# A decoder step on one core: seven half-tile products in place of eight in the up projection of the second token half

## What is computed

```
g = x @ w_gate                       # 1024 x 2816
g_c = depthwise_causal_conv(g, w_dw) # 3 taps along the tokens
y = (gelu(g_c) * (x @ w_up)) @ w_down
```

## Time and profile before

| what | us |
|---|---|
| median of 3 runs (lowest, highest) | 3045.91 (3045.04, 3047.52) |
| span of the profiled execution | 3046.1 |
| PE busy | 3011.0 |
| DVE, ACT, POOL busy | 1858.8, 1354.2, 406.6 |
| up projection of half 1, each layer | 264.2 |

### The profile page before, as it was taken

How to read it: one execution, slowest core, us unless ns; L and a number is a source line. 1 busy time by engine, 2 the same in 40 slices (tenths; PEclk the granted TensorE clock), 3 DMA queues, 4 the chain that set the end, 5 groups by cost and what they waited for, 6 DMA issues and landing times.

```text
span 3046.1 us, 62013 instructions
## 1 busy us (share of the span) xinstructions
PE 3011.0 (99%) x24682; PEld 2625.4 (86%) x24682; DVE 1858.8 (61%) x2754; ACT 1354.2 (44%) x2427; POOL 406.6 (13%) x602
## 2 busy tenths in 40 slices
PE   8999999999999999999999999999999999999998
PEld 7887888888999998998777777777798888999998
DVE  6998677744655445534666666666567763555522
ACT  5344633333333333323676777776543333333322
POOL 0112000000000002220433333433100000000000
PEclk9999999999999999999999999999999999999999
DMA  4232233334333335556999999999623333333332
GB/s 132 72 86 79 84 90 97 97 107 121 98 97 91 90 105 182 177 164 213 344 390 404 396 404 395 404 403 393 229 84 97 97 95 113 113 105 89 89 109 85
DMA packets 483249, 534.60 MB, mean 176 GB/s; under 512 B 22241, under 2 KB 400474, under 8 KB 482888
## 3 DMA queue, kind: packets, MB, share of 16 engines
q1 hardware_dynamic: 467254, 482.90, 46.8%
q0 software_dynamic: 15616, 47.55, 4.7%
q10 hardware_dynamic: 92, 0.19, 0.0%
HBM read 486.84 MB, written 33.89 MB: 171 GB/s over the span
## 4 chain that ended last, share of the span: by engine, by line
PE 86%; DVE 9%; ACT 2%; issue 2%; DMA 1%; SPq 0%; DVEq 0%; ACTq 0%
PE PS L1149 59%; PE PS L2273 7%; PE PS L2309 4%; PE PS L2285 4%; DVE mT L952 4%; PE PS L2328 2%; PE PS L2347 2%; PE PS L2338 2%; DVE wlo L380 1%; PE PS L669 1%; ACT whi L375 1%; PE PS L1800 1%; PE PS L713 0%; PE PS L1022 0%; PE PS L623 0%
## 5 line engine op out<-in xcount | busy, mean ns | idle before, releaser
L375 ACT CAST whi<-raw 128x1024 fp32r<-128x1024 f32 (+1 forms) x368 | 379.5, 1031 | 917.9 <-PE PS L1149 884.2
L380 DVE TENSOR_TENSOR wlo<-raw,whi 128x1024 fp32r<-128x1024 f32 (+1 forms) x368 | 442.7, 1203 | 556.5 <-ACT whi L375 543.4
L1149 PE MATMUL PS<-xfh,whi 128*128 128x512 f32 (+2 forms) x2240 | 618.9, 327 | 1.0 <-DVE wlo L380 0.9
L1149 PE MATMUL PS<-xfh,wlo 128*128 128x512 f32 (+2 forms) x2240 | 615.2, 326 | 0.0
L1149 PE MATMUL PS<-xfl,whi 128*128 128x512 f32 (+2 forms) x2240 | 613.5, 325 | 0.0
L1149 PEld LDWEIGHTS PS<-xfh,whi 128*128 128x128 f32 x2240 | 379.1, 188 | 35.5 <-issue 3.4
L1149 PEld LDWEIGHTS PS<-xfl,whi 128*128 128x128 f32 x2240 | 379.6, 188 | 32.4 <-issue 0.5
L1149 PEld LDWEIGHTS PS<-xfh,wlo 128*128 128x128 f32 x2240 | 378.5, 188 | 33.0
L2273 PE MATMUL PS<-ident,kr 128*128 128x128 f32 x2048 | 277.3, 276 | 2.6 <-ACT kt L2443 2.6
L2273 PEld LDWEIGHTS PS<-ident,kr 128*128 128x128 f32 x2048 | 224.7, 140 | 39.0 <-issue 37.2
L2536 DVE COPY kt<-PS 128x512 f32<-128x512 f32 x256 | 172.6, 681 | 129.8 <-PE PS L2273 128.1
(11 more groups left out here) (380 smaller groups left out, 5348.6 us busy)
## 6 DMA issues: line engine op xcount, KB each, us to landing
kr<-in_cache_k SPq DMA_DIRECT2D x256, 512.0 KB, 7.5
vr<-in_cache_v SPq DMA_DIRECT2D x256, 512.0 KB, 7.2
raw<-in_ffn_w_gate SPq DMA_DIRECT2D x88, 512.0 KB, 3.8
raw<-in_ffn_w_up SPq DMA_DIRECT2D x88, 512.0 KB, 3.8
raw<-in_ffn_w_down SPq DMA_DIRECT2D x64, 512.0 KB, 3.7
raw<-in_ffn_w_down SPq DMA_DIRECT2D x32, 384.0 KB, 3.4
raw<-in_conv_w_glu SPq DMA_DIRECT2D x16, 512.0 KB, 4.2
raw<-in_conv_w_out SPq DMA_DIRECT2D x16, 512.0 KB, 3.7
```

The lines of the kernel that those rows point to most:

```text
L375: nc.scalar.copy(whi[b][:, 0:blocks_of(t), :], raw[t % RAWS][:, 0:blocks_of(t), :]).then_inc(w_hi, 1)
L380: nc.vector.tensor_tensor(wlo[t % RAWS][:, 0:n, :], raw[t % RAWS][:, 0:n, :], whi[b][:, 0:n, :].bitcast(F32), ALU.subtract).then_inc(w_lo, 1)
L1149: mm = nc.tensor.matmul(PS[:, s + c, 0:c1 - c0], stationary(wt, t, kw + k), x(k0 + k)[:, c0:c1], start=start and k == 0 and wt is whi and ...
```

## The change

Blocks 3 to 19 of half 1 in both layers are worked as a pair of tiles: the 2 x 2 matrix of weight quarters (A11, A12 the gate tile's row blocks 0 to 3 and 4 to 7, A21, A22 the value tile's) times the 2 x 2 matrix of input quarters (4 row blocks, 272 columns), by seven products (`product`, 4 x 3 matmuls of 272 columns) in place of eight.

- The weight sums S1 = A21 + A22, S3 = A11 - A21, S2 = A22 - S3, S4 = A12 - S2 are made on POOL (`weight_sum`, one 128 x 512 tensor_tensor each), one block ahead. ACT rounds the seven left operands (S1, S3, S2, S4, A11, A12, A22; `weight_high`, 128 x 512 each); DVE makes the low parts of S1, A11, S2, A12 (`weight_low`), POOL those of S3, S4, A22 (`weight_low_pool`).
- Four input sums (1088 columns each) are made once per layer: DVE scales the input again in float32 (`x32`), POOL subtracts (`input_sums`), ACT rounds and DVE takes the low parts in block 1.
- Partial sums are joined by ACT copies of 272 columns (P5 to `c5`, two from PSUM to PSUM, and the first half of the gate to `gx`) and DVE additions (`paired_value_second`: 272 columns of PSUM and `c5`; `paired_gate_second`: 240 and 32). The taps, GELU and rounding of block f run while block f + 1 is on PE.
- Products P3 and P4 of a block run within the next block.
- Residual steps of the first half come every second block (2, 4, ... 16) instead of blocks 2 to 9.
- To make room, the finished products of blocks 0 to 7 go to DRAM and come back before the down projection, and so does the second half of the residual `hT` (POOL's DMA queue; both loads behind the last paired block). The scratch for DMA descriptors is set to 4096 bytes.
- Other blocks are worked as before.

The core of the diff:

```diff
+FS0, FS1 = 3, 20
+NG = FS1 - FS0
+HK = KB // 2
+KEPT = 8
...
+        def paired_sp(sp, layer, g):
+            f, G = FS0 + g, NG * layer + g
+            gate, value = A["ffn_w_gate"][layer], A["ffn_w_up"][layer]
...
+            if g >= 1:
+                sp.wait_ge(sg_s, SG_S + s_count(layer, g - 1, "S3"))
+            sp.dma_start(sA21[:], cols(value, f, 0, HK)).then_inc(sg_ld21, 16)
+            if g >= 3:
+                sp.wait_ge(w_used, used_count(layer, g - 3, "P4"))
+            sp.dma_start(sA22[g % 3][:], cols(value, f, HK, HK)).then_inc(sg_ld22[g % 3], 16)
+            if g >= 2:
+                sp.wait_ge(sg_p, SG_P + p_count(layer, g - 2, "P2"))
+            sp.dma_start(sA[g % 2][:], cols(gate, f)).then_inc(sg_ld[g % 2], 16)
...
+        def product(pe, bank, hi, lo, xh_, xl_, opened):
+            for j in range(HK):
+                for wt, x in ((hi, xh_), (hi, xl_), (lo, xh_)):
+                    mm = nc.tensor.matmul(PS[:, bank, 0:HC], wt[:, j, :], x(j), start=opened and j == 0 and wt is hi and x is xh_,
+                                          stop=j == HK - 1 and wt is lo, skip_group_check=True)
+            return mm
...
+        def paired_rest_pe(pe, layer, g, which):
+            G, s = NG * layer + g, g % 2
+            q, x, y = banks(layer, g)
+            if which == "P3":
+                pe.wait_ge(sg_l, SG_L + l_count(layer, g, "S4"))
+                product(pe, x, s4_hi, s4_lo[s], lower(HK, HC, xfh), lower(HK, HC, xfl), False).then_inc(w_used, 1)
+            else:
+                pe.wait_ge(sg_l, SG_L + l_count(layer, g, "A22"))
+                pe.wait_ge(sg_c22, SG_C22 + G + 1)
+                product(pe, y, A22_hi, sA22_lo[g % 3], sums(3, t_hi), sums(3, t_lo), False).then_inc(w_used, 1)
...
+        def paired_pe(pe, layer, g):
+            f, G, s = FS0 + g, NG * layer + g, g % 2
+            q, x, y = banks(layer, g)
+            u0 = uses[f"up{layer}1"]
+            if g == 0:
+                pe.wait_ge(sx_l, SX_L + 4 * (layer + 1))
+                pe.wait_ge(f_p, FB * (2 * layer + 1) + f - 1)
+            else:
+                read_by_act(pe, u0 + 2 * (f - 2) if g >= 2 else u0 + 2 * (f - 2))
+            pe.wait_ge(sg_d, SG_D + d_count(layer, g, "S1"))
+            product(pe, q, s1_hi, s1_lo, sums(0, t_hi), sums(0, t_lo), True).then_inc(sg_p, 1)
+            if g >= 1:
+                paired_rest_pe(pe, layer, g - 1, "P3")
+            pe.wait_ge(sg_d, SG_D + d_count(layer, g, "A11"))
+            pe.wait_ge(sg_c5, SG_C5 + G + 1)
+            product(pe, q, A11_hi, sA_lo[s][:, 0:HK], lower(0, 0, xfh), lower(0, 0, xfl), True).then_inc(sg_p, 1)
+            if g >= 1:
+                paired_rest_pe(pe, layer, g - 1, "P4")
+            pe.wait_ge(sg_d, SG_D + d_count(layer, g, "S2"))
+            pe.wait_ge(sg_sx, SG_SX + G + 1)
+            product(pe, x, s2_hi, s2_lo[s], sums(2, t_hi), sums(2, t_lo), False).then_inc(sg_p, 1)
+            pe.wait_ge(sg_d, SG_D + d_count(layer, g, "A12"))
+            product(pe, q, A12_hi, sA_lo[s][:, HK:KB], lower(HK, 0, xfh), lower(HK, 0, xfl), False).then_inc(sg_p, 1)
+            pe.wait_ge(sg_l, SG_L + l_count(layer, g, "S3"))
+            pe.wait_ge(sg_sy, SG_SY + G + 1)
+            product(pe, y, s3_hi, s3_lo[s], sums(1, t_hi), sums(1, t_lo), False).then_inc(sg_p, 1)
+            if g == NG - 1:
+                paired_rest_pe(pe, layer, g, "P3")
+                paired_rest_pe(pe, layer, g, "P4")
 
         def up_pe(pe, layer, half):
             t0, u0 = first[f"up{layer}{half}"], uses[f"up{layer}{half}"]
             hi, lo, _ = ffn_x[half]
             for f in range(FB):
...
+        def paired_act(act, layer, g):
+            f, G = FS0 + g, NG * layer + g
+            F = FB * (2 * layer + 1) + f
+            q, x, y = banks(layer, g)
+            gp = gx[f % 2]
+            weight_high(act, layer, g, "S3")
+            act.wait_ge(sg_p, SG_P + p_count(layer, g, "P5"))
+            if g >= 2:
+                act.wait_ge(sg_c12, SG_C12 + G - 1)
+            nc.scalar.copy(c5[g % 2][:], PS[:, q, 0:HC]).then_inc(sg_c5, 1)
+            weight_high(act, layer, g, "S4")
+            if g + 1 < NG:
+                weight_high(act, layer, g + 1, "S1")
+            act.wait_ge(sg_p, SG_P + p_count(layer, g, "P1"))
+            if g >= 2:
+                act.wait_ge(sg_c12, SG_C12 + G - 1)
+            else:
+                act.wait_ge(f_p, F - 1 if g == 0 else F - 1)
+            nc.scalar.copy(PS[:, x, 0:HC], PS[:, q, 0:HC]).then_inc(sg_sx, 1)
+            if g + 1 < NG:
+                weight_high(act, layer, g + 1, "A11")
+            weight_high(act, layer, g, "A22")
+            act.wait_ge(sg_p, SG_P + p_count(layer, g, "P6"))
+            act.wait_ge(f_p, F - 1 if g >= 1 else F)
+            nc.scalar.copy(PS[:, y, 0:HC], PS[:, x, 0:HC]).then_inc(sg_sy, 1)
+            if g >= 1:
+                paired_gel(act, F - 1)
+            if g + 1 < NG:
+                weight_high(act, layer, g + 1, "S2")
+            act.wait_ge(sg_p, SG_P + p_count(layer, g, "P2"))
+            act.wait_ge(f_cv, F - 1)
+            nc.scalar.copy(gp[:, 2:2 + HC], PS[:, q, 0:HC]).then_inc(ps_a, 1)
+            if g + 1 < NG:
+                weight_high(act, layer, g + 1, "A12")
+            if g >= 1:
+                product_high(act, f - 1, F - 1)
+
+        def paired_gel(act, F):
+            act.wait_ge(f_cv, F + 1)
+            act.wait_ge(f_p, F)
+            nc.scalar.activation(gel[:], cv[0][:], ACT.Gelu_apprx_tanh).then_inc(f_gel, 1)
+
...
+            def paired_product(g):
+                f, G = FS0 + g, NG * layer + g
+                _, _, y = banks(layer, g)
+                full = p_full(1, kept(1, f))
+                dve.wait_ge(f_gel, FB * (2 * layer + 1) + f + 1)
+                dve.wait_ge(sg_c22, SG_C22 + G + 1)
+                then(nc.vector.tensor_tensor(full[:, HC:NH], gel[:, HC:NH], full[:, HC:NH], ALU.mult))
+                dve.wait_ge(w_used, used_count(layer, g, "P4"))
+                own()
+                nc.vector.tensor_tensor(full[:, 0:HC], gel[:, 0:HC], PS[:, y, 0:HC], ALU.mult).then_inc(f_p, 1)
+
+            def paired_dve(g):
+                f = FS0 + g
+                if g >= 1:
+                    paired_value_second(g - 1)
+                    paired_gate_second(g - 1)
+                else:
+                    low(f - 1)
+                if g + 1 < NG:
+                    weight_low(dve, layer, g + 1, "S1")
+                if g >= 1:
+                    paired_conv(g - 1)
+                if g + 1 < NG:
+                    weight_low(dve, layer, g + 1, "A11")
+                post_part(f)
+                if g >= 1:
+                    paired_product(g - 1)
+                if g + 1 < NG:
+                    weight_low(dve, layer, g + 1, "S2")
+                if g >= 1:
+                    low(f - 1)
+                if g + 1 < NG:
+                    weight_low(dve, layer, g + 1, "A12")
+
+            def paired_end():
...
+                parts_stored(dve, layer, 0)
+                dve.wait_ge(w_used, t0 + 2)
+                for k in range(KB):
+                    nc.vector.scalar_tensor_tensor(out=x32[:, k, :], in0=hT[:, k, tokens(1)], scalar=vec[:, k, V_FFN_PRE + layer:V_FFN_PRE + layer + 1],
+                                                   in1=rs_x[:], op0=ALU.mult, op1=ALU.mult).then_inc(sx_x, 1)
...
+                    for n_ in range(4):
+                        dve.wait_ge(sx_h, SX_H + 4 * layer + n_ + 1)
+                        nc.vector.tensor_tensor(t_lo[:, n_], t32[:, n_], t_hi[:, n_].bitcast(F32), ALU.subtract).then_inc(sx_l, 1)
...
+                if i == 0 and half == 1:
+                    pe.wait_ge(p_out, P_OUT + 32 * KEPT * (layer + 1))
...
+                pool.wait_ge(p_h, KB * (4 * layer + 2))
+                for k in range(KB):
+                    pool.dma_start(h_dram[:, k, tokens(1)], hT[:, k, tokens(1)]).then_inc(h1_out, 16)
...
+        def input_sums(pool, layer):
+            a11, a12 = x32[:, 0:HK, 0:HC], x32[:, 0:HK, HC:NH]
+            a21, a22 = x32[:, HK:KB, 0:HC], x32[:, HK:KB, HC:NH]
+            pool.wait_ge(sx_x, SX_X + KB * (layer + 1))
+            nc.gpsimd.tensor_tensor(t32[:, 0], a12, a11, ALU.subtract).then_inc(sx_t, 1)
+            nc.gpsimd.tensor_tensor(t32[:, 1], a22, a12, ALU.subtract).then_inc(sx_t, 1)
+            pool.wait_ge(sx_t, SX_T + 4 * layer + 1)
+            nc.gpsimd.tensor_tensor(t32[:, 2], a22, t32[:, 0], ALU.subtract).then_inc(sx_t, 1)
+            pool.wait_ge(sx_t, SX_T + 4 * layer + 3)
+            nc.gpsimd.tensor_tensor(t32[:, 3], a21, t32[:, 2], ALU.subtract).then_inc(sx_t, 1)
+
...
             if half == 1:
                 pool.wait_ge(n_lo, KB * (X_FFN[layer] + 2))
+                pool.wait_ge(sx_x, SX_X + KB * (layer + 1))
+                for k in range(2):
+                    parts_back_pool(pool, layer, 0, k, ring_e)
+                input_sums(pool, layer)
```

(75 more changed lines are left out.)

315 lines of the change are left out of this document (270 added, 45 removed).

## The result

The changed kernel takes 3204.0 us (median of 4, 3198.8 to 3205.9) against 3046.5 for the kernel before in the same measurement: ratio 1.0515, 95% interval 1.050 to 1.053. It is slower by 157 us where the prediction had 55. The profiled execution took 3202.5 by its own time, its span is 3200.8, against 3046.1 before.

A forecast was written before the change was run, and what follows sets the result against it. PE, 99% busy, bounds the kernel before; in paired blocks DVE and POOL holding each other would set the pace. 3046.1 + 36 (blocks) + 17 (start) + 2 (end) = 3101 us; range 3068 to 3125, wider 3000 to 3140, all high ends 3167.

The forecast's parts named there:

- the ring: Loop of in-order waits through POOL, ACT and DVE, closing once per paired block: 9.9 us undisturbed, 12.5 with mutual holding.
- the hand schedule: One paired block laid out from durations, DVE and POOL holding each other: 12.5 us, 13.9 with a residual step.
- first rival: Paired blocks: PE stays the limit, every block 10.5 us, the whole 2999 us; chance 0.17.
- rival 4: Paired blocks: seven products don't shorten PE, matmuls would take 143 ns each; the whole 3051 us; chance 0.02.
- the block term: 34 paired blocks over two layers, mean 13.1 us against 12.02: +36 us, bounds +19 and +77.
- The first tap, a tensor_scalar with one input, passes.: Paired block: DVE's first tap is not held by POOL's low S4, which runs to 5.5 us in the schedule.
- The third rival: Paired blocks: DVE's tensor_scalar tap is held too, blocks 13.7 and 15.1 us, the whole 3142; chance 0.15.
- One of these takes 1.09 when undisturbed.: Paired block: one POOL 128x512 tensor_tensor takes 1.09 us; the rounding form was taken as 1.27.
- The terms of 8.5: Start of stage, per layer: PE waits 8.5 us, from 2.6 late plus 4 x 1.9 held, less 1.0 slack.
- The splits of the input sums lie against pauses: nothing: Block 1: splits of 4.4 us on ACT and 5.2 on DVE cost nothing against pauses of 4.4 and 4.6.
- They fit: End of stage: reloads of eight kept products fit under blocks 20 and 21, 24 us; refilling PE costs 1 us a layer.
- The upper bound of 10: End of stage, per layer: 10 us put in the upper bound for uncovered reloads, also covering the smaller descriptor scratch.

## Why the prediction was right and wrong

**Right: the direction and the mechanism.** The blocks got longer because DVE and POOL hold each other, and the ring closes where it was drawn, POOL pausing for ACT's cast S3. From the end of the taps to POOL's next low the hand schedule had 3.4 us, and 4.8 with a residual step; the trace has 3.37 (969.60 to 972.96) and 4.99. PE did get shorter as costed: 10.55 in place of 10.5 once nothing holds it up (first rival's price, and its condition did not hold). Nothing speaks for rival 4.

**Wrong: the size of the block term, in the stretch from POOL's low S3 to the end of the taps.** It takes 11.2 us where 9.1 was laid out. These 2.1 us per block, some 70 over 34 blocks, are all that the block term was short by (103 for 36). The schedule had six of POOL's seven operations over by 8.75 us and put the seventh, sum S4, behind the taps. In the trace all seven run in a row, 10.3 us, before the taps end. Three assumptions stand behind that:
- "The first tap, a tensor_scalar with one input, passes." It does not: 1508 ns for 487. The third rival had this, with sum S4 falling into the taps, and priced it at 13.7 and 15.1. The Trainium skill (SBUF — State Buffer, "Who interferes with whom") counts tensor_scalar and copy among the operations that can take the shared pair, and the traces agree, at 1508 and 889 ns for 487 and 164. The prediction cited it and gave it 0.15. But the held tap is not by itself the 1.2 us that the rival gives it: with that tap on ACT the blocks fell by 0.56 us only, and POOL's seven operations still ran in a row.
- "One of these takes 1.09 when undisturbed." That was a multiplication. POOL's subtraction of 128x512 takes 1.29 alone, the rounding form as well. The four sums were 0.2 short each. 13.7 + 0.8 and 15.1 + 0.8 are 14.5 and 15.9, the measured blocks; that this sum fits is arithmetic, since no run changed the length of POOL's sums alone.
- Small copies had no hold in the schedule, and 32-column taps none of their own. A copy of 2 columns and two of the three small taps each take a whole turn, but by the run without those taps (0.5 us) that is cheap: another operation would have had the turn.

**Start: 17.9 and 17.2 us, not 8.5.** The terms of 8.5, written out (2.6 + 4 x 1.9 - 1.0), add up to 9.2. PE waited 11.35 us for the third tile's low. The make-up of the term was right and the hold under-sized: 9.65 us in the taps (11.38 less 1.73) where it had 7.6, and 1.6 + 9.65 is 11.25. "The splits of the input sums lie against pauses: nothing" was wrong by 4.0 us, PE's wait for the first paired low behind t_lo (7.1 us, 793.98 to 801.08, where 5.2 was laid out; POOL's sums run beside it). Those two waits make 15.4 in layer 0; the other 2.5 are about what the half clock costs after the long wait (granted 0.82 from 775 to 790 with PE busy throughout, so some 2.7), a size read from the windows and tested by no run.

**End: 9.8 and 8.7 us, not 1.** "They fit" looked at the reloads and not at what queues behind them. The upper bound of 10 held it.

The sum of the upper ends, 3167, was too low by 37 us, and the range with it. 26 of these lie in the blocks (103 for 77; 34 x 0.8 is 27, by POOL's 1.29) and 11 in the start (35 for 24).
